# The right half of the memory attention's output projection in float32r halves, its weights split before the attention and the first rows' transposes moved into the last matmul group

## The reference, cut to what matters

```python
def memory_attn(h, mem, w_q, w_kv, w_o):
    q = (h @ w_q).reshape(B, S, MEM_HEADS, MEM_HEAD_DIM)      # 4 heads of 256
    k, v = jnp.split(mem @ w_kv, 2, axis=-1)
    ...
    s = jnp.einsum('bshd,bmhd->bhsm', q, k).astype(jnp.float32) * (MEM_HEAD_DIM ** -0.5)
    p = jax.nn.softmax(s, axis=-1).astype(v.dtype)
    o = jnp.einsum('bhsm,bmhd->bshd', p, v).reshape(B, S, D_MODEL)
    return o @ w_o
...
        y = memory_attn(x, mem, mem_w_q[i], mem_w_kv[i], mem_w_o[i])
        x = layer_norm(ALPHA * x + y, ln_g[i, 2], ln_b[i, 2])
        y = swiglu(x, ffn_w_gate[i, 1], ffn_w_up[i, 1], ffn_w_down[i, 1])
```

## Time and profile before

| | before |
|---|---|
| median of three runs | 2744.1 us |
| lowest and highest | 2741.22 and 2744.46 us |
| the profiled execution's own time | 2738.89 us |
| its span in the trace | 2736.9 us |
| PE busy | 2628.1 us, 96% |
| DVE, ACT, POOL busy | 57%, 41%, 5% |
| mean granted clock of PE | 0.995 |

### The profile page before, as it was taken

The page is one execution under the profiler, slowest core; times in us unless marked ns, Lnnn a source line. Parts: engine busy times, 40 slices in busy tenths (PEclk is TensorE's granted clock), DMA queues, the critical chain, the costliest instruction groups (busy, mean ns, idle before and its releaser), DMA issues.

```text
span 2736.9 us, 38996 instructions
## 1 busy us (share of the span) xinstructions
PE 2628.1 (96%) x16908; PEld 2104.0 (77%) x16908; DVE 1563.8 (57%) x1694; ACT 1117.8 (41%) x1350; POOL 149.9 (5%) x121
## 2 busy tenths in 40 slices
PE   9999999999999999998899999999999899999998
PEld 7996687998989787997565779975667688885477
DVE  5456646456464635456874654458746447564377
ACT  4333534334434543434321454343214345353355
POOL 0002000000011100002011000010110000000000
PEclk9999999999999999999999999999999999999999
DMA  6654335657545254554532435545224257577786
GB/s 231 220 200 139 108 139 184 213 196 226 189 154 185 93 185 159 201 179 144 163 106 78 163 143 201 188 160 167 92 65 155 93 195 282 189 249 258 261 294 229
DMA packets 227774, 484.24 MB, mean 177 GB/s; under 512 B 11708, under 2 KB 45116, under 8 KB 227412
## 3 DMA queue, kind: packets, MB, share of 16 engines
q1 hardware_dynamic: 227604, 481.75, 51.2%
HBM read 477.01 MB, written 2.95 MB: 175 GB/s over the span
## 4 chain that ended last, share of the span: by engine, by line
PE 81%; DVE 11%; ACT 3%; DMA 2%; issue 2%; POOL 1%; SPq 0%; DVEq 0%; ACTq 0%; POOLq 0%
PE psum L732 19%; PE psum L432 12%; PE psum L434 11%; PE psum L433 11%; PE psum L435 10%; PE psum L479 5%; DVE weight_ring_low_halves L427 3%; PE psum L3358 2%; PE psum L2468 2%; PE psum L2554 1%; PE psum L619 1%; ACT weight_high_halves L421 1%; POOL small L653 1%; DVE stage_area_halves L610 1%; PE psum L3288 1%
## 5 line engine op out<-in xcount | busy, mean ns | idle before, releaser
L427 DVE TENSOR_TENSOR weight_ring_low_halves<-weight_ring,weight_high_halves 128x2048 fp32r<-128x2048 f32 (+2 forms) x334 | 737.1, 2213 | 493.8 <-ACT weight_high_halves L421 493.4
L421 ACT ACTIVATE weight_high_halves<-weight_ring 128x2048 fp32r<-128x2048 f32 (+2 forms) x347 | 640.1, 1853 | 536.0 <-PE psum L434 236.6
L432 PE MATMUL psum<-weight_high_halves,stage_area_halves 128*128 128x512 f32 (+4 forms) x1542 | 601.2, 390 | 21.5 <-DVE stage_area_halves L610 10.9
L434 PE MATMUL psum<-weight_high_halves,stage_area_halves 128*128 128x512 f32 (+4 forms) x1542 | 589.1, 382 | 0.0
L732 PE MATMUL psum<-stage_area_halves,weight_high_halves 128*128 128x256 f32 x2880 | 510.4, 281 | 0.0
L433 PE MATMUL psum<-weight_ring_low_halves,stage_area_halves 128*128 128x512 f32 (+4 forms) x1322 | 504.9, 382 | 0.0
L732 PEld LDWEIGHTS psum<-stage_area_halves,weight_high_halves 128*128 128x128 f32 x2880 | 441.9, 189 | 1.1
L732 PE MATMUL psum<-stage_area_halves,weight_ring_low_halves 128*128 128x256 f32 x1440 | 405.5, 282 | 0.0
L432 PEld LDWEIGHTS psum<-weight_high_halves,stage_area_halves 128*128 128x128 f32 x1542 | 290.1, 188 | 122.9 <-issue 50.2
L434 PEld LDWEIGHTS psum<-weight_high_halves,stage_area_halves 128*128 128x128 f32 x1542 | 290.0, 188 | 58.5
L435 PE MATMUL psum<-weight_ring,stage_area 128*128 128x512 f32 x704 | 309.5, 598 | 5.1 <-issue 4.1
(11 more groups left out here) (336 smaller groups left out, 2719.4 us busy)
## 6 DMA issues: line engine op xcount, KB each, us to landing
weight_ring<-in_ffn_w_gate SPq DMA_DIRECT2D x44, 1024.0 KB, 5.1
weight_ring<-in_ffn_w_up SPq DMA_DIRECT2D x44, 1024.0 KB, 5.1
weight_ring<-in_ffn_w_down SPq DMA_DIRECT2D x44, 1024.0 KB, 4.8
weight_ring<-in_w_in SPq DMA_DIRECT2D x36, 1024.0 KB, 7.3
weight_ring<-in_moe_wd SPq DMA_DIRECT2D x27, 1024.0 KB, 4.9
weight_ring<-in_moe_wu SPq DMA_DIRECT2D x25, 1024.0 KB, 6.6
weight_ring<-in_moe_wg SPq DMA_DIRECT2D x22, 1024.0 KB, 6.7
weight_ring<-in_mem_w_kv SPq DMA_DIRECT2D x16, 1024.0 KB, 5.1
```

The lines of the kernel that those rows point to most:

```text
L421: act.raw.activation(self.high_half(name), self.in_slot(name), ACT.Copy).then_inc(*act.mark("high_halves", ("high", name)))
L427: v.raw.tensor_tensor(self.low_half(name), self.in_slot(name), self.high_half(name), ALU.subtract).then_inc(*v.mark("low_halves", ("halves ...
L432: pe.raw.matmul(out, a[1], w[0], start=start, stop=False)
L434: return pe.raw.matmul(out, a[0], w[0], start=False, stop=stop)
```

## The change: what it does

The weights of column block 1 of the memory outputs are planned as split pieces, in both layers. ACT splits the two pieces between the copies of query pairs 2 and 3, and DVE makes their low halves ahead of the attention. After the attention ACT copies the attention's output into the high part, row tile by row tile, in the place of the memory tokens' halves, and DVE subtracts. PE takes the output projection group by group, the groups of block 0 in plain float32 and those of block 1 in halves, and the transposes of the first rows are issued after the fourth of the eight k steps of the last group. The two more pieces in the ring of high halves shift all the later ones by two slots, and the place of the reciprocals in layer 1's mixer (`key_inverse`) moves by two slots.

```diff
@@ proj_tensor
-    ..., before=(None, ()), rows=range(MT), only=None):
+    ..., before=(None, ()), rows=range(MT), only=None, inside_last=()):
...
             for k in range(kts):
+                if k == 4 and inside_last and (b, m) == (len(pr["cols"]) - 1, MT - 1):
+                    self.turn_tensor(pe, inside_last)
                 w = self.weights(pe, (tag, b, k // 4))
@@ First.__init__
-        self.key_inverse = net.branch_gates[:, 0:2 * MT * P].rearrange("p (i t) -> p i t", t=P)
+        self.key_inverse = net.spare_halves[:, 0:2 * MT * P].rearrange("p (i t) -> p i t", t=P)
...
-            st["mo"] = net.plan_proj(f"mem{i}_o", ins["mem_w_o"][i], blocks(D), KT)
+            st["mo"] = net.plan_proj(f"mem{i}_o", ins["mem_w_o"][i], blocks(D), KT, split=(1,))
@@ First.tensor
-            net.proj_tensor(pe, st["mo"], oT, self.out_bank, [done, done], rows_first=True, before_last=by_rows(n + 3)[0])
+            for m in range(MT):
+                net.proj_tensor(pe, st["mo"], oT, self.out_bank, [done, done], only=[(0, m)])
+                pe.wait_ge(*pe.at(("recalled_halves", i, m)))
+                net.proj_tensor(pe, st["mo"], lambda k, m: pick(self.memT_halves, k, m), self.out_bank, only=[(1, m)],
+                                inside_last=by_rows(n + 3)[0])
@@ First.scalar
-            net.projT_copy(act, st["mq"], range(4), net.qT, ["scalar"])
+            net.projT_copy(act, st["mq"], range(4), net.qT, ["scalar"], range(3))
+            net.split_scalar(act, st["mo"]["pieces"][2:])
+            net.projT_copy(act, st["mq"], range(4), net.qT, ["scalar"], [3])
             attn_scalar(net, act, f"mem{i}", self.mem_heads(i))
+            act.wait_ge(*act.at(*[(f"mem{i}", "oT", g) for g in range(4)]))
+            for m in range(MT):
+                rows = slice(m * P, (m + 1) * P)
+                act.raw.activation(self.memT_halves[0][:, :, rows], net.oT[:, :, rows], ACT.Copy).then_inc(*act.mark("recalled_high", ("recalled_high", i, m)))
             self.rows_scalar(act, n + 3, st["ffn1"]["gate_up"][0])
@@ First.vector
             net.split_vector(v, st["mq"]["pieces"][2:])
+            net.split_vector(v, st["mo"]["pieces"][2:])
             attn_vector(net, v, f"mem{i}", self.mem_heads(i), 1)
+            for m in range(MT):
+                rows = slice(m * P, (m + 1) * P)
+                v.wait_ge(*v.at(("recalled_high", i, m)))
+                v.raw.tensor_tensor(self.memT_halves[1][:, :, rows], net.oT[:, :, rows], self.memT_halves[0][:, :, rows], ALU.subtract).then_inc(
+                    *v.mark("recalled_low", ("recalled_halves", i, m)))
```

More of the change, by code:

```diff
@@ L480, in passes, with proj_tensor @@
                 yield i, k, mm
-    def proj_tensor(self, pe, pr, lhsT, bank, need=(), turn_1=(), rows_first=False, before_last=(), before=(None, ()), rows=range(MT), only=None):
+    def proj_tensor(self, pe, pr, lhsT, bank, need=(), turn_1=(), rows_first=False, before_last=(), before=(None, ()), rows=range(MT), only=None, inside_last=()):
         tag, kts = pr["tag"], pr["kts"]
```

## The result

| | before | changed |
|---|---|---|
| median of five runs each | 2744.1 us | 2758.45 us |
| lowest to highest | 2741.22 to 2747.19 | 2757.08 to 2759.93 |
| the profiled execution, its span | 2738.89, 2736.9 us | 2757.08, 2755.3 us |
| mean granted clock of the profiled execution | 0.995 | 0.989 |

The ratio is 1.0057, with a 95% interval of 1.0046 to 1.0068: 14 us slower, forecast 15.

The account below looks back on a forecast made before the run. PE, busy 96% of the span, was taken to bound the kernel. Per layer +6.8 (late piece) +2.2 (clock) −1.4 (saving kept) = +7.6, both +15.2, so 2759.3 us from the median 2744.1; range 2751 to 2766.

Parts of the forecast that it names:

- Part 1, the products: Output projection on PE: products in halves save 1.33 us a group, 2.66 a layer, 5.3 in all.
- Part 2, the late piece: Ahead of the attention: ACT's split of late-loaded piece (1,1) delays query pair 3's copy by 6.8 us a layer.
- Part 3, the clock: First scores after PE's wait: the clock falls and costs 2.2 us a layer, bounds 0 and 3.5.
- the 0.2 for the first transposes: Part of the clock's 2.2 us: 0.2 added in case the low stretch reaches the first transposes.
- The row at 1257.28: Profile row of the kernel before, used to forecast the clock: after 5.42 us idle, granted clock 0.53.
- Part 4, the give-back: Around the output projection: DVE's late norm of row 1 leaves 1.4 of the 2.66 us saved a layer.
- The sum: Whole kernel: +6.8 +2.2 −1.4 = +7.6 us a layer, +15.2 in both, 2759.3 us.
- (a), no fall of the clock: First scores: clock stays, or falls only before they start; +10.8 us, 2754.9; chance 0.17.
- (b), the piece in time: Ahead of attention: last piece isn't late, PE never stops, only the saving is left, 2741.3 us; chance 0.05.
- (c): Worse: 3.5 us for the clock, no saving kept, or landing after 7.3 us; +20.6, 2764.7; chance 0.10.
- The signs: Profile: late load, L421 waiting 7 to 9 us, PE idle over 7, clock near 0.5, late row 1 norm.

Follow-up runs that it names:

- The wait alone: Kernel before, with one edit: ACT waits until output piece (1,1) is loaded ahead of query pair 3's copy; 2755.64 us, ratio 1.0049.
- the filler: Changed kernel plus 8 unread float32 products on PE between the queries' projection and the first scores, both layers; 2752.96 us, ratio 1.0036.
- the kernel with no wait: Changed kernel with output piece (1,1) split behind the attention on ACT and DVE, same run as the first experiment; 2736.77 us, ratio 0.9980.
- the two kernels without a wait: The first experiment and the second experiment, both with piece (1,1) split behind the attention; 2736.77 us and 2734.22 us.
- the first experiment: Changed kernel with the split of output piece (1,1) moved behind the attention on ACT and DVE; 2736.77 us, ratio 0.9980.
- the second experiment: The first experiment with the first rows' transposes back ahead of the last group; 2734.22 us, ratio 0.9977.
- the last one: The first experiment, transposes in mid-group, with ACT and DVE taking gate piece (0,1) ahead of the first rows' transposes; 2736.24 us, ratio 0.9977.
- the transposes alone: Changed kernel, late split left, with only the first rows' transposes put back ahead of the last group; 2753.81 us, ratio 1.0042.

## Why the prediction was right

- **Part 1, the products.** 2.66 us a layer by the sum; 2.65 is what the stage loses where nothing is given back (57.66 less 55.01). In the changed kernel a plain group and one in halves take 12.50 us together (408.79 to 421.29), so 5.6 for the second with 6.89 for the first. The Trainium skill ("FP8 and Floating Point Precision", section TensorE Precision Notes) says that true FP32 takes four passes; my estimate from it, a pass at the 0.231 us of a float32r matmul, would have had the stage lose 3.7. What the traces refute is that price and not the number of passes: 0.861 us is 3.7 float32r matmuls, and it would be four passes of 0.215, which no run here can tell from two records of 0.431.
- **Part 2, the late piece.** 6.8 us forecast, 6.80 and 6.92 measured; the load is issued when the projection ends, lands 5.0 us later, and ACT's split and the copy follow. The wait alone, put into the kernel before, makes the loss, and moving the one split away ends it.
- **Part 3, the clock.** 2.2 forecast. Against the filler, 1.8 in layer 0; against the kernel with no wait, 2.3 in layer 1; 1.6 to 2.6 over all the executions with the wait. The third head's scores came 5.79 us after the first (389.79 to 395.58), I had worked out 6.0. The fourth head's were as late as the third's (1.78), so the 0.2 for the first transposes was not there in layer 0. The row at 1257.28 was a fair measure. The fall itself came behind all eight waits of 5.80 to 7.74 us that the profiles show ahead of the scores; it did not come where PE had work in the same wait. The Trainium skill ("TensorE: Matmul & The Clock Gate", section HAM oscillation — how this bites in real kernels) says that PE, left waiting for a DMA, is throttled again and starts the next work cold; these traces agree (0.50 in the wait and 0.56 behind it, in layer 0), and in the earlier trace rows the same came behind a wait for DVE.
- **Part 4, the give-back.** 1.25 forecast, 1.28 measured (56.29 less 55.01), by the chain that was named: turn copies, gate piece (0,1), norm of row 1. Its two parts were forecast at 0.8 (the norm) and 0.4 (the low half of the second up piece); from the starts of the two kernels without a wait they are 0.76 (row 1's transposes at 35.83 and 35.07 us behind the first L435) and 0.5 (the eight low matmuls behind them). The brackets, 0.60 and 0.17, show less than that: here a bracket understates what such a wait costs.
- **The sum.** +15.2 forecast from the rows, 15.1 in the two stages, 14.35 between the medians. It came out well in part by luck: single executions of one kernel lie several microseconds apart, the two profiled spans differ by 18.4, and the clock's share alone ran from 1.6 to 2.6 a layer.
- **The rivals.** (a), no fall of the clock, is out by the windows and by the filler; (b), the piece in time, is out by SP's row; it describes what the first experiment made true by moving the split. (c) kept too little, 1.4 us of the saving was really there, and its 3.5 for the clock was not reached in any layer (2.6 at most).
- **The signs.** They are there but for one number: ACT's L421 waited 6.7 us for the load and not 7 to 9. The prediction's own working gives 6.6 (from 379.9, when piece (1,0) is split, to 386.5), so the sign was written down wrongly and the term was right.

## What to carry to other kernels

Work that looks free because an engine idles there is only free if its input can be there too: for a weight out of a ring, ask which piece gave up the slot and when, before looking at the engine's idle time. One instruction that waits in an in-order queue holds all that stands behind it, here the copy on which the next stage starts. And before moving a group of instructions into the middle of another, follow what stands behind their copies on the helper engines; the same move was free or cost 1.3 us by whether one split came before or after.

## What the runs showed of the hardware that was not expected

The price of the clock did not grow with the wait. 5.0 and 5.3 us more of idle time cost 2.5 and 1.8 us of slow scores on top; 6.8 to 7.0 us more cost between 1.6 and 2.6. The same kernel's two layers differed by up to 0.9, so a single stage doesn't give this price closely.

The clock also falls, or doesn't, at a place that this change doesn't touch, in the mixer between the two stages. Busy time by windows in three kernels: the changed one, the second experiment, the last one:

```profile
920.00:924.00 4.00, 4.00 (x8) 1.70 (x7) 3.00 (x2) 4.00 (x3) 0.00 (x0) 0.68 0.00 0
```

```profile
904.00:908.00 4.00, 3.48 (x10) 1.45 (x7) 1.48 (x2) 3.00 (x2) 0.00 (x0) 0.65 0.00 0
```

```profile
908.00:912.00 4.00, 3.34 (x11) 1.71 (x12) 0.76 (x2) 2.28 (x2) 0.00 (x0) 0.73 0.00 0
```

In the profiled executions of the kernel before, of the first experiment, of the filler and of the transposes alone the clock is 1.00 in all this stretch; in the wait alone and in the second profile of the changed kernel it falls too, so in five profiles of nine. From the end of layer 0's stage to the start of layer 1's the first two of these took 566.24 and 566.26 us, the second experiment 567.96 and the last 567.94: 1.7 us more with the fall. That is the size of what one would like to measure here. And executions of one and the same kernel differ like this too: of the eleven of the first experiment the two lowest (2733.02 and 2733.65 us) had a mean granted clock of 0.995, the three highest (2740.5, 2741.33 and 2741.5) 0.991, 0.993 and 0.992. This is why a difference of 2.5 us between two kernels was settled by the length of a stage and not by their times. Whether the fall in the mixer belongs to an execution or to a kernel wasn't tried: only the changed kernel was profiled twice, and the clock fell there both times. The late copy does not decide it, since with it the clock fell here in two kernels and stayed in two (the filler and the transposes alone).

And a fall need not cost anything. Ahead of the wait of the earlier trace rows 16 gate matmuls took 5.51 us in the changed kernel's profile, at a granted clock of 0.76 over 1260 to 1267, and 3.97 in the kernel before. The wait for DVE behind them was shorter by as much, 3.87 us and not 5.42, and from the transposes ahead of those matmuls to the ones behind that wait it is 17.00 us in both kernels.
